# Two streams at two stage transitions: by-token norms, context scaled on VectorE and added on GpSimd, x's products first

## The chip, the core and the metric

The kernel runs on one core of a Trainium2 chip. The metric is the device time of one execution in microseconds (us), the median of three runs. A core has five engines that matter here, each with its own instruction queue: TensorE (PE, matmuls; its weight loads are shown apart as PEld), VectorE (DVE), ScalarE (ACT), GpSimd (POOL) and SyncE (SP, which here only issues the DMAs that load weights). They are ordered among each other by semaphores alone. SBUF holds the operands, PSUM (eight banks of 128 x 512 fp32) the results of matmuls. `fp32r` is the split format in which the kernel makes its matmul operands.

## The reference

Two transformer blocks in fp32, one after the other, on one sequence of 512 tokens with 1024 features. The change lies in the second block, which has two streams: `x` (512 tokens) and `ctx` (256 tokens), with the same weights but gains of their own. Cut to what matters (`shf`, `scf` are a shift and a scale per feature, made from the condition vectors; `_x` and `_c` are the two streams'):

```python
# layer 0
yx, yc = conv_module(hx, ...), conv_module(hc, ...)
x   = x   + g_x * rmsnorm(yx, norm_g[0, 1])        # post-norm and residual
ctx = ctx + g_c * rmsnorm(yc, norm_g[0, 1])
fx = rmsnorm(x,   norm_g[0, 2]) * (1 + scf_x) + shf_x   # next norm
fc = rmsnorm(ctx, norm_g[0, 2]) * (1 + scf_c) + shf_c
x   = x   + gf_x * rmsnorm((silu(fx @ w1) * (fx @ w3)) @ w2, norm_g[0, 3])
ctx = ctx + gf_c * rmsnorm((silu(fc @ w1) * (fc @ w3)) @ w2, norm_g[0, 3])
# layer 1
hx = rmsnorm(x,   norm_g[1, 0]) * (1 + sc_x) + sh_x
hc = rmsnorm(ctx, norm_g[1, 0]) * (1 + sc_c) + sh_c
# keys, values: hx and hc @ wk, wv;   queries: hx @ wq;   then attention, post-norm, ffn of x alone
```

## The kernel before, in words

Activations stand transposed: features on the 128 partitions in KD = 8 chunks, tokens along the free axis (`X` is 8 x 512, `XC` 8 x 256). Every matmul operand is split into a high and a low fp32r part, and each product is made of three matmuls (lines 435 to 437: high weights by high activations, high by low, low by high). A weight matrix is cut into slabs, 1024 rows by 128 columns as a rule. SP loads a slab into one of three `raw` buffers, ACT makes `Wh` from it (L2090), and DVE (L1313) or POOL (L2592) makes `Wl = raw - Wh`; `by_pool` says which. There are three `Wh`/`Wl` pairs, so a slab's `Wh` waits until the products of the slab three before it are done. `ahead(key)` on ACT and DVE makes the parts up to two slabs ahead of `key`.

All five programs are written out by hand as Python functions that emit instructions in order; no scheduler moves them. So an instruction waits for all that stands ahead of it on its engine, and PE's order is that of the calls.

Two places have this form, and are called transition 1 (convolution module to the ffn of layer 0) and transition 2 (that ffn to the attention inputs of layer 1):

1. The post-norm. PE sums the squares of y (`norm_stats`), a root is taken by token: PE leaves one number per token and partition (`token_stat`, L569: the squares are the stationary operand, a column of ones the moving one, so each of the matmuls has one column), ACT and DVE work on 128 x 4 numbers (`small`, L2138, L2141, L1383 to L1392), and PE spreads them again with transposes (`token_rows`, L581) into a "row" in PSUM. `fill_in=(1, 4)` puts one matmul of no use (128 x 512, `keep_warm`, L625) before the transposes and four behind.
2. DVE scales y by row and gain (L1410) and adds it to X (L1481), chunk after chunk, first x's eight, then ctx's eight (`post_norm`).
3. The next norm. ACT squares the new X (L2125) as its chunks come, then ctx's; there are two `sq` buffers. PE sums them with `stat` (L557: ones as the stationary operand, 512 or 256 columns), so the sum comes out spread over all partitions, and the root is taken on 128 x 512 numbers (DVE, four instructions over 512 columns). WARM_AFTER adds four `keep_warm` matmuls.
4. `norm_to_h`: DVE scales chunk c of X (L1410), ACT adds the shift and rounds (L2163, `Hh`), DVE takes the low part (L1427, `Hl`). Then the same for ctx (`hc_h`, `hc_l`).
5. `linear_pair_both`: PE makes the products of the first two slabs with x, chunk by chunk as `Hl` comes, then those with ctx. The third slab and the others follow by `linear_both`, x and ctx in turn.

In the attention inputs (jobs k2_0, k2_1, v2_0, v2_1, then q2_0 to q2_7) each key and query slab is followed on PE by `head_stat` (L557 and L911, the swapped pairs for the rotation). DVE does the rotation (L1681 to L1685), the head's root (L1383 to L1392), the scaling (L1706) and the low parts (L1731, L1736), and ahead of each the `Wl` of a later slab. At transition 0 (into the convolution) the kernel already has the by-token norm for both streams and `linear_trio_both`, which makes three slabs' products with x before any with ctx.

Of the kernel before, what the change touches and what calls it, by code (L numbers as in the profile page):

```python
# [24 lines left out]
P = 128  # L25
# [68 lines left out]
def write(nc, a, out, tally):  # L94
# [285 lines left out]
    WARM = 8  # L380

    def by_pool(key):

        return key[0] in BLOCK_1_SLABS or key[0:2] == ("dn", 1)
# [9 lines left out]
    BY_TOKEN = [t for t in SUMMED if t != ("post", ("ffn", 1, "x"))]  # L394
# [3 lines left out]
    def _(pe):  # L398
# [98 lines left out]
        def linear_trio_both(tag, *three_jobs):  # L497
# [16 lines left out]
            for i in range(KD):  # L514
                pe.wait_ge(*ready("h_low", tag, i))
                for job, w in ws:
                    products(job, w, i, "x")
            take(*three_jobs[2])
# [9 lines left out]
            tally.h_reader[0] = ws[2][0]  # L528

# [70 lines left out]

        def norm_stat(tag, c, n):
# [15 lines left out]


# [146 lines left out]
        def ffn_both():  # L765

            tag, w2 = ("f", 0, "x"), a["ffn_w2_2"][0]
            for lo, hi in F_GROUPS:
                for f in range(lo, hi):
                    w = {x: a["ffn_w%s_2" % x][0, :, f * P:(f + 1) * P] for x in "13"}  # L770
                    if f == 0:
                        linear_pair_both(tag, *((("up" + x, 0, "x", f), w[x], "split") for x in "13"))
                    else:
                        for x in "13":
                            linear_both(("up" + x, 0, "x", f), w[x], ("f", 0, "c"))
# [17 lines left out]
            token_rows(*(("post", ("ffn", 0, s)) for s in "xc"), fill_in=(1, 4))  # L793
# [31 lines left out]
        def conv_both():  # L825
# [32 lines left out]
            token_rows(*(("post", ("conv", s)) for s in "xc"), fill_in=(1, 4))  # L858
# [22 lines left out]
        def attention_inputs():  # L881
# [3 lines left out]
            linear_pair_both(tag, *((("k2", "x", p), wk(p), "split") for p in range(2)))  # L885
            jobs = attention_jobs
            head_stat(jobs[0])
            for i in range(2, len(jobs) + 1):
# [6 lines left out]
                one = jobs[i - 1]  # L895
                if one[0] == "v2":
# [235 lines left out]
        def gqa_attend():  # L1132
# [63 lines left out]
            token_rows(("post", ("att", "x")), fill_in=(1, 4))  # L1196
# [57 lines left out]
        for s in ("x", "c"):  # L1254
            pre(("f", 0, s), NS[s])
        ffn_both()
        for s in ("x", "c"):
            pre(("n", 1, s), NS[s])
# [26 lines left out]
    def _(dve):  # L1285
# [126 lines left out]
        def norm_to_h(tag, n, g, sh, gains=None, ring="one", rooted=False):  # L1412
# [17 lines left out]
            for c in range(KD):  # L1430
# [6 lines left out]
                if c > 0:  # L1437
                    low(c - 1)
            low(KD - 1)

        def norms_to_h(kind, l, ring="both"):

            for s in ("x", "c"):
                norm_to_h((kind, l, s), NS[s], lambda c: col(2, l, s, 7 if kind == "f" else 6, c),
                          lambda c: col(2, l, s, 3 if kind == "f" else 0, c), ring=ring)
# [56 lines left out]
        def conv_both():  # L1502
# [74 lines left out]
            post_norms(("conv",), 0, 8)  # L1577

        def post_norms(tag, l, what):

            for s in ("x", "c"):
                rstd(("ss", ("post", (*tag, s))), NS[s], D)
            for s in ("x", "c"):
                post_norm((*tag, s), NS[s], YB[:, :, 0:SEQ] if s == "x" else YB[:, :, SEQ:],
                          lambda c: col(2, l, s, what, c), "both")

        def ffn_both():

            norms_to_h("f", 0)
# [22 lines left out]
            post_norms(("ffn", 0), 0, 9)  # L1612
# [75 lines left out]
        def attention_inputs():  # L1688

            norms_to_h("n", 1, "one")  # L1690
# [380 lines left out]
    def _(act):  # L2071
# [88 lines left out]
        def norm_highs(tag, n, sh):  # L2160
# [5 lines left out]
        def norms_to_h(kind, l, ctx_ready):  # L2166
# [3 lines left out]
            norm_to_h(x, SEQ, lambda j: col(2, l, "x", what, j), lambda: squares_of_x(c, CTX, ctx_ready))  # L2170
            norm_to_h(c, CTX, lambda j: col(2, l, "c", what, j))
# [52 lines left out]
        def ffn_both():  # L2224

            norms_to_h("f", 0, lambda c: ready("x_new", ("conv", "c"), c))
# [63 lines left out]
        def attention_inputs():  # L2290

            norms_to_h("n", 1, lambda c: ready("x_new", ("ffn", 0, "c"), c))
# [243 lines left out]
        squares_of_x(("f", 0, "x"), SEQ, lambda c: ready("x_new", ("conv", "x"), c))  # L2536
# [221 lines left out]
```

## Time and profile before

| what | value |
|---|---|
| runs | 3268.11, 3269.18, 3278.44 us; median 3269.18 us |
| the profiled execution | 3274.4 us, of which the span of instructions is 3272.6 us |
| PE busy | 3154.5 us (96%) |
| DVE, ACT, POOL busy | 1568.0 us (48%), 1187.5 us (36%), 816.1 us (25%) |
| mean granted clock of TensorE | 0.985 of 2.4 GHz |

The page adds busy time by engine over the whole span; the chain follows back what ended last. A granted clock of 1.00 is TensorE at 2.4 GHz, 0.50 is 1.2 GHz, and values between are a mean over a stretch that holds both.

### The profile page before, as it was taken

To read this page: it belongs to the slowest core of one execution; us is meant where nothing else is said; L and a number is where in the kernel's file an instruction comes from. 1 tells how busy PE (TensorE), PEld (TensorE's weight loads), DVE (VectorE), ACT (ScalarE), POOL (GpSimd) and SP (SyncE) were. 2 spreads that over 40 slices of the span, in tenths; PEclk is the share of its full clock that TensorE was granted. 3 is DMA by queue.
4 is the path that set the end of the run, shared out by engine and by line. 5 is a ranking of instruction groups with operands and counts; after the bars stand their busy time and mean duration, and the time that the engine had idled before them with its cause. 6 is when DMAs were issued, how large, how long until landed. Compare 5 with 4: busy or idle time off the path is not lost.

```text
span 3272.6 us, 38617 instructions
## 1 busy us (share of the span) xinstructions
PE 3154.5 (96%) x15540; PEld 2480.0 (76%) x15540; DVE 1568.0 (48%) x2208; ACT 1187.5 (36%) x1764; POOL 816.1 (25%) x401
## 2 busy tenths in 40 slices
PE   6999999999999999999999899999999979999998
PEld 4657778887765777778877578888888658878887
DVE  3572146464376113333388644322334889653234
ACT  3443244243454223324321343111112558632223
POOL 4302436555320333444400000000000039400000
PEclk9999999999999999999999999999999989999999
DMA  6413436665430555463334211222221110122332
GB/s 238 128 43 110 143 95 194 213 200 165 129 116 1 169 178 167 144 191 92 95 103 121 53 49 55 65 65 65 65 64 52 40 38 1 39 71 87 106 89 79
DMA packets 429892, 337.21 MB, mean 103 GB/s; under 512 B 16637, under 2 KB 411223, under 8 KB 417428
## 3 DMA queue, kind: packets, MB, share of 16 engines
q1 hardware_dynamic: 428272, 334.23, 33.4%
q8 instruction: 124, 2.03, 0.2%
q0 software_dynamic: 1248, 0.46, 0.1%
q14 instruction: 52, 0.43, 0.0%
q10 hardware_dynamic: 196, 0.07, 0.0%
HBM read 319.58 MB, written 2.10 MB: 98 GB/s over the span
## 4 chain that ended last, share of the span: by engine, by line
PE 61%; DVE 5%; ACT 2%; issue 1%; SPq 1%; DMA 0%; POOL 0%; DVEq 0%; ACTq 0%
PE PS L435 17%; PE PS L436 17%; PE PS L437 17%; PE PS L871 1%; PE PS L557 1%; PE PS L1175 1%; PE PS L625 1%; PE PS L1144 1%; PE PS L670 1%; PE PS L1155 1%; PE PS L1176 1%; SPq L2681 1%; DVE both_tmp L1410 1%; DVE X L1481 0%; PE PS L569 0%
## 5 line engine op out<-in xcount | busy, mean ns | idle before, releaser
L435 PE MATMUL PS<-Hh,Wh 128*128 128x512 f32 x2208 | 874.9, 396 | 9.2 <-DVE Hl L1427 5.2
L2592 POOL TENSOR_TENSOR Wl<-raw,Wh 128x1024 fp32r<-128x1024 f32 (+2 forms) x254 | 617.8, 2441 | 989.6 <-ACT Wh L2090 989.6
L436 PE MATMUL PS<-Hl,Wh 128*128 128x512 f32 x2208 | 861.6, 390 | 0.0
L437 PE MATMUL PS<-Hh,Wl 128*128 128x512 f32 x2208 | 861.4, 390 | 0.0
L2090 ACT ACTIVATE Wh<-raw 128x1024 fp32r<-128x1024 f32 (+2 forms) x442 | 436.3, 988 | 394.5 <-PE PS L437 346.9
L435 PEld LDWEIGHTS PS<-Hh,Wh 128*128 128x128 f32 x2208 | 415.8, 188 | 116.7 <-issue 51.9
L437 PEld LDWEIGHTS PS<-Hh,Wl 128*128 128x128 f32 x2208 | 415.6, 188 | 87.9
L436 PEld LDWEIGHTS PS<-Hl,Wh 128*128 128x128 f32 x2208 | 416.0, 188 | 67.9 <-issue 3.4
L1313 DVE TENSOR_TENSOR Wl<-raw,Wh 128x1024 fp32r<-128x1024 f32 (+3 forms) x188 | 217.6, 1157 | 386.9 <-ACT Wh L2090 386.4
L1995 DVE SCALAR_TENSOR_TENSOR cv<-PS,vcols,cv 128x510 f32<-128x510 f32 (+1 forms) x176 | 123.7, 744 | 217.1 <-ACT cv L2511 217.1
L435 PE MATMUL PS<-g_h,Wh 128*128 128x512 f32 x528 | 206.7, 391 | 3.5 <-POOL Wl L2592 3.5
L2624 POOL CAST k_hi<-k_ctx 64x512 fp32r<-64x512 f32 x4 | 4.2, 1044 | 813.2 <-DVE k_ctx L1410 813.0
L437 PE MATMUL PS<-g_h,Wl 128*128 128x512 f32 x528 | 205.5, 389 | 0.0
L436 PE MATMUL PS<-g_l,Wh 128*128 128x512 f32 x528 | 205.5, 389 | 0.0
L435 PE MATMUL PS<-hc_h,Wh 128*128 128x256 f32 x576 | 162.7, 282 | 0.6 <-DVE hc_l L1469 0.5
L436 PE MATMUL PS<-hc_l,Wh 128*128 128x256 f32 x576 | 161.8, 281 | 0.0
L437 PE MATMUL PS<-hc_h,Wl 128*128 128x256 f32 x576 | 161.8, 281 | 0.0
L2639 POOL TENSOR_SCALAR p<-p,small 128x768 f32<-128x768 f32 x64 | 140.5, 2218 | 49.7 <-DVE small L2047 49.7
L557 PE MATMUL PS<-sq,cst 128*128 128x512 f32 (+2 forms) x228 | 111.0, 601 | 32.5 <-DVE stat_v L1383 16.2
L2511 ACT ACTIVATE cv<-PS,vcols 128x512 f32<-128x512 f32 x88 | 68.7, 780 | 191.8 <-PE PS L437 188.6
L435 PEld LDWEIGHTS PS<-hc_h,Wh 128*128 128x128 f32 x576 | 108.1, 188 | 21.9 <-DVE hc_l L1469 1.7
L436 PEld LDWEIGHTS PS<-hc_l,Wh 128*128 128x128 f32 x576 | 108.1, 188 | 19.9
(384 smaller groups left out, 4785.3 us busy)
## 6 DMA issues: line engine op xcount, KB each, us to landing
raw<-in_ffn_w SPq DMA_DIRECT2D x108, 512.0 KB, 3.6
mod_w<-in_w_mod SPq DMA_DIRECT2D x48, 1024.0 KB, 5.0
raw<-in_w_up SPq DMA_DIRECT2D x88, 512.0 KB, 4.7
mod_w<-in_w_ada SPq DMA_DIRECT2D x40, 1024.0 KB, 4.9
raw<-in_w_in SPq DMA_DIRECT2D x62, 512.0 KB, 3.9
UQ<-U SPq DMA_DIRECT2D x128, 99.4 KB, 2.2
raw<-in_w_down SPq DMA_DIRECT2D x32, 384.0 KB, 5.1
raw<-in_conv_w_pw SPq DMA_DIRECT2D x24, 512.0 KB, 4.2
```

Source lines behind the costliest of these rows:

```text
L435: pe.matmul(o, wh, xh, start=start, stop=False, skip_group_check=True)
L436: pe.matmul(o, wh, xl, start=False, stop=False, skip_group_check=True)
L437: return pe.matmul(o, wl, xh, start=False, stop=stop, skip_group_check=True)
L557: mm = pe.matmul(bank(job, n), const(matrix)[lo:hi, :], SQ[i][lo:hi, 0:n], start=first, stop=final, skip_group_check=True)
L625: pe.matmul(PS[:, b, :], const("ident"), cst[:, 0:512], start=True, stop=True)
L670: mm = pe.matmul(PS[32 * j:32 * j + b, bank_of[job], :], cact[b][:, r, :], w[:, 512 * j:512 * (j + 1)], start=r == 0, stop=r == KD - 1, sk ...
L1313: dve.tensor_tensor(low, src, high.bitcast(F32), ALU.subtract).then_inc(*mark("w_low", k))
L1995: ins = dve.scalar_tensor_tensor(o, bank(ups[s])[:, 0:SEQ - lag], vec(("w_conv", l), tap * 2 * FC + s * FC + f), o, ALU.mult, ALU.add)
L2090: act.activation(high, src, ACT.Copy).then_inc(*mark("w_high", k))
L2511: act.activation(cv[f % 2][s][:, :], bank(job), ACT.Identity, bias=vec(("b_conv", l), s * FC + f), scale=vec(("w_conv", l), 2 * 2 * FC + s ...
L2592: pool.tensor_tensor(low, src, high.bitcast(F32), ALU.subtract).then_inc(*mark("w_low_pool", one[0]))
L2639: pool.tensor_scalar(p2[n % 5][:, :], p2[n % 5][:, :], ri2[n % 5], None, ALU.mult)\
```

## The change

The roots of the norms that follow at transitions 1 and 2 are taken by token, for x and ctx (`BY_TOKEN`). Each chunk's squares go through PE by themselves (`chunk_stat`: one-column matmuls, in the place of L557). DVE scales ctx's y in place in YB (eight instructions), and POOL adds it to XC (`add_context`). DVE takes x's next norm before ctx's; ACT squares four chunks of ctx ahead of x's `Hh`, four between them, and takes ctx's root behind the sixth. PE takes the last four chunks of ctx between x's products. Three slabs (instead of two) have x's products made first. The third slab's low part is made by POOL (`THIRD_SLABS`). In the attention inputs `head_stat` of k2_1 moves behind the products of v2_1. The post-norms' `fill_in` goes from (1, 4) to (1, 2), at a third place too, the post-norm of the attention; `pre` of the two norms, with its four `keep_warm`, goes.

```diff
-    BY_TOKEN = [t for t in SUMMED if t != ("post", ("ffn", 1, "x"))]
+    BY_TOKEN = ([t for t in SUMMED if t != ("post", ("ffn", 1, "x"))]
+                + [(*t, s) for t in (("f", 0), ("n", 1)) for s in "xc"])
+    THIRD_SLABS = ("up1", 0, "x", 1), ("v2", "x", 0)
 # PE
+        def into(tag, *three_jobs):
+            c_tag = (*tag[:-1], "c")
+            for c in range(KD):
+                chunk_stat(tag, c, "stat")
+            token_rows(tag, fill_in=(0, 0), own_banks=True)
+            for c in range(4):
+                chunk_stat(c_tag, c, "mod")
+            keep_warm(1)
+
+            def after(i):
+                if i in (1, 3):
+                    for c in (i + 3, i + 4):
+                        chunk_stat(c_tag, c, "mod")
+                if i == KD - 2:
+                    token_rows(c_tag, fill_in=(0, 0), own_banks=True)
+
+            linear_trio_both(tag, *three_jobs, after=after)
...
-            token_rows(*(("post", ("ffn", 0, s)) for s in "xc"), fill_in=(1, 4))
+            token_rows(*(("post", ("ffn", 0, s)) for s in "xc"), fill_in=(1, 2))
...
-            linear_pair_both(tag, *((("k2", "x", p), wk(p), "split") for p in range(2)))
+            into(tag, *((("k2", "x", p), wk(p), "split") for p in range(2)),
+                 (jobs[2], a["attn_wv_2"][0, :, 0:P], "split"))
             head_stat(jobs[0])
-            for i in range(2, len(jobs) + 1):
+            for i in range(3, len(jobs) + 1):
...
                 one = jobs[i - 1]
+                if i == 3:
+                    head_stat(jobs[1])
 # DVE
+            post_norm((*tag, "x"), SEQ, YB[:, :, 0:SEQ], lambda c: col(2, l, "x", what, c), "both")
+            for c in range(KD):
+                one = scaled(YB[:, c, SEQ:], YB[:, c, SEQ:], col(2, l, "c", what, c), CTX, r=bank(row, CTX))
+                one.then_inc(*(empty(row) if c == KD - 1 else mark("ctx_scaled", tag, c)))
 # ACT
+            ahead(first_slab(x))
+            squares_of_x(x, SEQ, lambda j: ready("x_new", (*post, "x"), j))
+            root(("ss", x), SEQ)
+            for j in range(4):
+                square_of_c(j)
+            norm_highs(x, SEQ, lambda j: col(2, l, "x", what, j), between)
+            norm_highs(c, CTX, lambda j: col(2, l, "c", what, j))
 # POOL
+            pool.tensor_tensor(low, src, high.bitcast(F32), ALU.subtract).then_inc(*mark("w_low_pool", third))
+            for c in range(KD):
+                pool.tensor_tensor(XC[:, c, :], XC[:, c, :], YB[:, c, SEQ:], ALU.add).then_inc(*mark("ctx_new", post, c))
```

PE at transition 1, before: the post-norm's transposes (L581), fill (L625), squares' sums of x and ctx, fill, first products.

```order
L625 MATMUL PS<-cst 128x512
L581 MATMUL PS<-cst,small 128x128 x6
L625 MATMUL PS<-cst 128x512 x4
L557 MATMUL PS<-sq,cst 128x512 x8
L557 MATMUL PS<-sq,cst 128x256 x8
L625 MATMUL PS<-cst 128x512 x4
L435 MATMUL PS<-Hh,Wh 128x512
```

The same place in the changed kernel (its L591 is `token_stat`, L603 the transposes, L665 the fill).

```order
L665 MATMUL PS<-cst 128x512
L603 MATMUL PS<-cst,small 128x128 x6
L665 MATMUL PS<-cst 128x512 x2
L591 MATMUL PS<-cst,sq 128x1 x32
L603 MATMUL PS<-cst,small 128x128 x4
L591 MATMUL PS<-cst,sq 128x1 x8
L665 MATMUL PS<-cst 128x512
L437 MATMUL PS<-Hh,Wh 128x512
```

Sixteen wide matmuls became 40 of one column (the other eight stand between the products), and of nine fill matmuls four are left.

PE in the attention inputs, before: `head_stat` of k2_1 (its operand is heads_in_144) stands behind v2_0's products and ahead of v2_1's, which are the last three rows' kind.

```order
L437 MATMUL PS<-hc_h_61,Wl 128x256
L557 MATMUL PS<-sq,cst 128x512
L911 MATMUL PS<-heads_in_144,cst 128x512
L435 MATMUL PS<-Hh,Wh 128x512
L436 MATMUL PS<-Hl,Wh 128x512
L437 MATMUL PS<-Hh,Wl 128x512
L435 MATMUL PS<-hc_h_61,Wh 128x256
```

The same pair in the changed kernel: v2_1's products end in the first row, and behind the pair the turns of v2_0 (heads_in_145) follow at once, then q2_0's products.

```order
L439 MATMUL PS<-hc_h_61,Wl 128x256
L579 MATMUL PS<-sq,cst 128x512
L956 MATMUL PS<-heads_in_144,cst 128x512
L968 MATMUL PS<-cst,heads_in_145 128x128 x4
L968 MATMUL PS<-cst,vt_c_137 128x128 x2
L437 MATMUL PS<-Hh,Wh 128x512
```

The rotation's operand of k2_1 now comes one slab later.

## Rows read from the trace of the kernel before

**Rows 1.** The page: busy us of the engines, share of the span, instructions

```profile
PE 3154.5 (96%) x15540; PEld 2480.0 (76%) x15540; DVE 1568.0 (48%) x2208; ACT 1187.5 (36%) x1764; POOL 816.1 (25%) x401
```

**Rows 2.** Chain of waits, transition 1: start us, us, what

```profile
1945.64 1.41 DVE both_tmp L1410 x2
...
1956.94 0.39 DVE both_tmp L1410
...
1967.29 3.43 PE PS L625 x8
1970.73 0.23 PE PS L435
...
1987.27 0.23 PE PS L435
```

**Rows 3.** Chain of waits, transition 2

```profile
2532.26 1.41 DVE both_tmp L1410 x2
2533.67 0.60 DVE X L1481
2534.27 0.66 DVE both_tmp L1410
...
2541.87 0.64 ACT sq L2125
2542.55 2.00 PE PS L557 x4
...
2555.66 0.23 PE PS L435
...
2574.03 0.86 PE PS L911 x2
...
2583.22 0.86 PE PS L557 x2
```

**Rows 4.** Weight loads of one-column matmuls: start us, us, engine, line, shapes, count

```profile
2524.01 0.97 PEld L569 LDWEIGHTS PS<-cst,stat_v 128*128 128x128 f32 x8 [0.58 <-issue]
2525.82 1.78 PEld L569 LDWEIGHTS PS<-cst,sq 128*128 128x128 f32 x8 [0.83 <-ACT sq L2125]
2528.33 0.97 PEld L569 LDWEIGHTS PS<-cst,sq 128*128 128x128 f32 x4
```

**Rows 5.** Windows: stretch, length, busy us of each engine, granted clock, DMA

```profile
2523.30:2527.50 4.20, 3.05 (x19) 2.79 (x19) 1.80 (x3) 1.12 (x3) 0.00 (x0) 0.77 0.00 0
2527.50:2529.20 1.70, 1.70 (x9) 1.70 (x10) 0.65 (x4) 0.47 (x2) 0.00 (x0) 0.50 0.00 0
2532.20:2536.00 3.80, 3.80 (x11) 1.89 (x10) 3.73 (x6) 1.07 (x2) 0.00 (x0) 0.97 0.00 0
2612.00:2614.00 2.00, 2.00 (x6) 1.53 (x5) 1.90 (x4) 1.42 (x3) 0.00 (x0) 0.50 0.00 0
```

**Rows 6.** A root by token: timelines of ACT and DVE, transition 1

```profile
1941.57 0.26 ACT L2138 ACTIVATE small<-PS,cst 128x4 f32<-128x4 f32 x1
...
1942.57 0.16 DVE L1392 SCALAR_TENSOR_TENSOR small<-small 128x4 f32<-128x4 f32 x1
```

**Rows 7.** Timeline of DVE in the attention inputs, with its idle time before

```profile
2584.97 0.69 DVE L1681 TENSOR_TENSOR tmp<-PS,turnS 128x512 f32<-128x512 f32 x1 [2.84 <-PE PS L911]
...
2604.64 1.22 DVE L1313 TENSOR_TENSOR Wl<-raw,Wh 128x1024 fp32r<-128x1024 f32 x1
2607.65 0.69 DVE L1681 TENSOR_TENSOR tmp<-PS,turnS 128x512 f32<-128x512 f32 x1 [1.80 <-PE PS L911]
...
2619.86 0.69 DVE L1681 TENSOR_TENSOR tmp<-PS,turnS 128x512 f32<-128x512 f32 x1 [3.29 <-PE PS L911]
2622.80 1.77 DVE L1386 TENSOR_TENSOR stat_t<-stat_y 128x512 f32<-128x512 f32 x1
```

**Rows 8.** Windows there, later

```profile
2640.00:2660.00 20.00, 18.07 (x66) 11.72 (x64) 19.37 (x28) 10.61 (x16) 0.00 (x0) 1.00 0.27 79
```

**Rows 9.** Groups of POOL by form: shapes, count, busy us, mean ns, idle before

```profile
L2592 POOL TENSOR_TENSOR Wl<-raw,Wh 128x1024 fp32r<-128x1024 f32 x186 | 487.3, 2628 | 842.1 <-ACT Wh L2090 842.1
L2634 POOL TENSOR_TENSOR v_parts<-v_ctx,v_parts 128x256 fp32r<-128x256 f32 x2 | 2.7, 1328 | 0.2
```

More of the change, by code:

```diff
@@ L599, in summed_stat, with chunk_stat @@
                 tally.square_free[ev] = lambda: full(job)
+        def chunk_stat(tag, c, ring="work"):
+            job, ev = ("ss", tag), (tag, c)
+            if c == 0:
+                begin(job, ring)
+            pe.wait_ge(*ready("squares", ev))
+            i = len(tally.squares) % 2
+            tally.squares.append(ev)
+            mm = token_stat(job, SQ[i], NS[tag[-1]], c == 0, c == KD - 1)
+            if c == KD - 1:
+                mm.then_inc(*fill(job))
+                tally.square_free[ev] = lambda: full(job)
+            else:
+                mm.then_inc(*mark("squares_used", ev))
+                tally.square_free[ev] = lambda: ready("squares_used", ev)
         def norm_stat(tag, c, n):
@@ L616, in keep_warm @@
         def keep_warm(count=WARM):
+            if count == 0:
+                return
             b = turn_of["work"]
@@ L857, in conv_both @@
             norm_stats(("post", ("conv", "x")), KD - 1)
-            token_rows(*(("post", ("conv", s)) for s in "xc"), fill_in=(1, 4))
+            token_rows(*(("post", ("conv", s)) for s in "xc"), fill_in=(1, 2))
         def quad_taps(j):
@@ L1438, in norm_to_h @@
                     low(c - 1)
+                if c == KD - 2 and after_6:
+                    after_6()
             low(KD - 1)
[L1441 to L1445, printed above, removed]
         def mod_out(b, l):
@@ L2164, in norm_highs, with norms_to_h, square_of_c, between @@
                    .then_inc(*mark("h_high", tag, c))
-        def norms_to_h(kind, l, ctx_ready):
+                after(c)
+        def norms_to_h(kind, l, post):
             x, c = (kind, l, "x"), (kind, l, "c")
             what = 3 if kind == "f" else 0
-            norm_to_h(x, SEQ, lambda j: col(2, l, "x", what, j), lambda: squares_of_x(c, CTX, ctx_ready))
-            norm_to_h(c, CTX, lambda j: col(2, l, "c", what, j))
+            def square_of_c(j):
+                act.wait_ge(*ready("ctx_new", post, j))
+                square((c, j), XC[:, j, :], CTX)
+            def between(j):
+                if 1 <= j <= 4:
+                    square_of_c(j + 3)
+                if j == 5:
+                    root(("ss", c), CTX)
+            ahead(first_slab(x))
+            squares_of_x(x, SEQ, lambda j: ready("x_new", (*post, "x"), j))
+            root(("ss", x), SEQ)
+            if tally.h_before.get(x):
+                act.wait_ge(*full(tally.h_before[x]))
+            for j in range(4):
+                square_of_c(j)
+            norm_highs(x, SEQ, lambda j: col(2, l, "x", what, j), between)
+            norm_highs(c, CTX, lambda j: col(2, l, "c", what, j))
         def squares_of_x(tag, n, ready_of):
```

52 lines of the change are left out of this document (29 added, 23 removed).

## The prediction

> **What bounds the kernel now.** I read the page first. PE is busy in 96% of the span [rows 1], so a gain must come from PE's waits, its half clock or its extra work, and there is little of each. Then I followed the chain of waits through the two transitions. At transition 1 it leaves PE at 1945.64, where DVE starts the post-norm, and comes back to products at 1970.73, which is 25.1 us; the last 3.43 us are the fill [rows 2]. At transition 2 the same stretch is 2532.26 to 2555.66, 23.4 us [rows 3]. DVE's pairs of L1410 and L1481 take 0.66 + 0.60 = 1.26 us a chunk, so x's post-norm is about 10 us of it, in both kernels. The windows show the clock, and the timeline of DVE shows what comes after: in the attention inputs DVE waits for PE until 2619.86 [rows 7] and from then on sets the pace (busy 19.37 of 20 us [rows 8]). So at transition 2 an earlier first product is worth nothing by itself; what counts is when DVE gets to 2619.86.
>
> **When x's squares are summed.** In the changed kernel PE passes each chunk as four one-column matmuls (eight loads in the trace, L569). At 2.4 GHz eight loads take 0.97 us, at 1.2 GHz 1.78 us [rows 4]. Less the last load's overlap that is a pitch of about 0.9 or 1.7 us a chunk, and for ctx's four loads (0.97 us at 1.2 GHz) 0.45 or 0.85. Against DVE's 1.26 us a chunk all hangs on the clock. The row that decides for me: from 2527.50 to 2529.20 PE is busy 1.70 of 1.70 us with such loads and their matmuls, and the granted clock is 0.50; in the 4.20 us before, mostly the same work, it fell (mean 0.77). It was back near 1.00 in the window with the four wide fill matmuls [rows 5]. I take it that the clock falls some 3 us behind the last wide matmul and stays at half over the rest of the sums. The Trainium skill (TensorE: Matmul & The Clock Gate, Part 1: The HAM clock gate) says that the gate goes by how busy the array has lately been. Taken at PE's busy share it would keep 2.4 GHz here; the row just named disagrees, and what it would give is rival A.
>
> At transition 2 two fill matmuls (0.86 us each, from 3.43 for four [rows 2]) behind 2532.4 end at 2534.1. Adds of X end 1.26 us apart from 2534.27, a square takes 0.64 more [rows 3]: chunks 0 and 1 are summed at full clock, chunk 2 starts at 2537.6, and six chunks at 1.7 us end at S = 2547.8. Before, the sums ended with the L557 at 2542.55 + 2.00 = 2544.55, so this is 3.2 us later. At transition 1 the fill begins at half clock and lasts longer; chunks 0 to 2 go at full clock, and five more from 1952.1 give S = 1960.6.
>
> **From S to the first product.** ACT's logarithm to DVE's root, by token: 1941.57 to 1942.57 + 0.16, so 1.2 us [rows 6], plus 0.1 of semaphore; before, this was four DVE instructions of 512 columns. Then PE at half clock: four transposes (0.85), four chunks of ctx (3.4), one fill matmul (1.7). The sum is 7.3 us. ACT's third and fourth squares of ctx wait for PE in there and x's first `Hh` waits behind them, but they end by S + 5.9 and are covered by the fill. Some 1.4 us of products at half clock lose half: 0.7 (0 to 2 us; the four restarts that I saw differ). So T' = S + 8.0: 1968.6 at transition 1, 2.1 us earlier than 1970.73; 2555.8 at transition 2, 0.1 us later than 2555.66. The row of x, its `Hh` and `Hl` on DVE are ready before. The cover for DVE's eight ctx scalings (3.1 us, from 0.39 each [rows 2]) is PE's slow sums; without it (rival A) they end 0.1 us before the root is due.
>
> **POOL.** The third slab's low part costs 2.63 us and lies beside x's post-norm, before any use. Eight adds of 256 columns are not in the trace: from 0.66 us each (a quarter of the 1024-column form, 2.63) to 1.33 us [rows 9]. I take the latter, the nearer shape. Eight are 10.6 us; the fourth, which ACT's fourth square needs, is ready 5.3 us after DVE's first scaling and so before S. Cost 0 (0 to 1 us). POOL's reads beside DVE can slow DVE: 1.77 us for an instruction that takes 0.69 otherwise [rows 7], but that hits DVE while it waits for PE's sums.
>
> **Transition 1, the sum.** Before, from 1970.73 to the third slab 16.5 us, and 8.3 for that slab (as v2_0 took, from 2574.03 + 0.86 to 2583.22 [rows 3]): 24.8. After, from T': 48 products with x at 0.227 us = 10.9 (a matmul of the chain shows 0.23 [rows 2]); four sums of ctx and two transposes between them 2.1 (1.8 and 0.3); 24 with x 5.5; 72 with ctx at half the columns 8.5. Together 27.0. ACT's root of ctx stands ahead of its seventh `Hh` and waits for PE's third stop; I find `Hl` 6 ready just as PE asks for it. Slab four needs the first pair's buffer: table load 1.28, gate 0.91, `Wh` 1.04, `Wl` 1.23 are 4.5 us against 5.7 us of products, so no stall. Net: -2.1 + 2.1 = 0.0 us.
>
> **Transition 2, the sum.** The trio ends at T' + 27.0, `head_stat` of k2_0 takes 0.86 + 0.86 [rows 3], v2_1 8.3, `head_stat` of k2_1 1.7. DVE's rotation of k2_1 thus starts at T' + 38.8; before, it started at 2584.97, which is T + 29.3. Behind it on DVE, in the order of the program: rotation, root and scaling 5.4, low parts of k2_0 2.8, `Wl` 1.2, v2_0 1.3, low parts of k2_1 2.8, `Wl` 1.2, v2_1 1.3, root of ctx's key 2.3, `Wl` 1.2: 19.6 us. It is also the stretch from 2584.97 to 2604.64 + 1.22 = 2605.86 [rows 7], 20.9 us, less two waits of 0.2 and 1.1 us that are gone because ACT is early. So the rotation of q2_0 starts at T' + 58.4 = 2614.2. Before, it waited for PE and started at 2607.65. That is 6.5 us later, and what follows keeps the distance: PE's sum for ctx's second key waits for DVE's reading of q2_0's bank, then q2_1's `head_stat`, then 2619.86 and DVE's own pace. PE will stand idle for about 2.3 us ahead of q2_1's products and 5 us ahead of q2_2's, the second as before at half clock afterwards (0.50 at 2612 [rows 5]). Net: +6.5 us.
>
> **The third `fill_in`.** Behind the attention PE is at full clock and DVE sets the pace; two fill matmuls fewer give 0 us.
>
> **Sum.** 0.0 + 6.5 = +6.5 on the profiled execution's 3274.4 gives 3280.9. That execution lies 5.2 us above the median of the runs, 3269.2, on which the forecast is put: 3275.7 us, 0.2% slower. A measurement of this kernel can't tell less than about 0.3% (9.8 us) from no change. With a clock loss of 0 to 2 us at each start, the fall of the clock a chunk earlier or later and POOL's 1 us, the forecast's own range is 3271 to 3280.
>
> **Rivals.**
> A. The one-column sums keep 2.4 GHz. Then DVE's pace ends the sums at about 2544.3, S to T' is 5.0 us (transposes 0.45, ctx 1.8, fill 0.86), T' is 2549.3 and 1962.4. Transition 1 gains 8.3 - 2.1 = 6.2; transition 2 has q2_0's rotation at 2607.7, as before, 0. That gives 3263.0. For it: PE is busy throughout; against: rows 5. It is also what the skill's rule at its word would make.
> B. DVE's queue in the attention inputs does not bind, because it is ahead by more than I count (its waits before were 2.84 and 1.80 us [rows 7]). Then transition 2 costs T' + 2.1, so 2.2 us: 3271.4.
> C. Slower than before: in the trio the one-column sums between x's products keep the clock at half until the pair is done. PE then takes 10.9 us more at each transition, DVE's `Hl` are no help, and transition 2 passes it on through k2_1: 3275.7 + 21.8 = 3297.5. It decides once the clock comes back more than 3.3 us later than I assume at both. Against: 12 wide products stand between two stops, and the clock rose with fill matmuls alone.
> D. The change doesn't do what it says: ctx's adds on POOL or the trio change nothing that is waited for, both transitions keep their length: 3269.
>
> **Chances.** Forecast 0.55, A 0.13, B 0.13, C 0.11, D 0.08. Faster by over 0.3% (under 3259.4) would need A and more at transition 2: 0.07. Slower by over 0.3% (above 3279.0): C and the upper edge of the forecast, 0.20. The same: 0.73. Range: 3263 (A) to 3281.
>
> **What the profile will show.** If the sums run at half clock: eight loads of a chunk 0.21 us apart from the third or fourth chunk on, granted clock 0.5 there, and x's first product 23 to 24 us after DVE's start of the post-norm at both transitions (25.1 and 23.4 before). If DVE's queue binds: PE waits for `Wl` of q2_1 and for DVE ahead of q2_2, and the rotation of q2_0 starts 82 us after the post-norm's start, in place of 75.4. The forecast is wrong if the first products come within 18 us, or if DVE waits for PE ahead of q2_0's rotation; it would be wrong for an unknown reason if the attention's products take another time than before.

## The result, and the profile after

The changed kernel takes 3279.88 us (median of 12 runs, 3278.38 to 3284.75), the kernel before 3273.94 in the same session (12 runs, 3268.11 to 3280.09). The ratio is 1.0021, with an interval of 1.0013 to 1.0029: 6.9 us slower, between 4.3 and 9.5. The difference of the two medians is 5.9 us. The forecast was 3275.7 us, a change of less than 0.3%, so the class is right. The time is 4.2 us above the forecast and lies 0.1 us inside the forecast's own range (3271 to 3280).

Executions of one kernel differ by several us in what lies ahead of the change: with identical code up to there, VectorE (DVE) starts the post-norm of transition 1 anywhere from 1941.4 to 1950.3 us in the traces of this case. So I compare stretches inside a trace. The first is from the start of DVE's post-norm to the second product of the gate (the `both_tmp` of L1598 before, L1641 after); the second from the same start at transition 2 to the rotation of q2_0, and on to the reduction of the first scores.

The lines have moved: L569 is L591 now, L581 L603, L625 L665, L911 L956, L1681 L1724. The chain of waits of the changed kernel at transition 1, in the columns of [rows 2]:

```profile
1941.44 1.41 DVE both_tmp L1451 x2
...
1947.94 8.71 PE PS L591 x40
...
1958.15 1.09 PE PS L603 x4
1959.24 3.21 PE PS L591 x16
1962.44 1.92 PE PS L665 x2
1964.36 0.43 PE PS L437
```

and at transition 2, beside [rows 3]:

```profile
2529.72 1.41 DVE both_tmp L1451 x2
...
2534.96 10.41 PE PS L591 x48
...
2546.70 1.08 PE PS L603 x4
2547.79 3.20 PE PS L591 x16
2550.99 1.92 PE PS L665 x2
```

Over the sums DVE has left the chain; it comes back only for the root. PE's one-column sums are in the chain with six chunks in a piece at transition 2 (eight entries a chunk): 10.41 / 6 = 1.74 us a chunk, where DVE delivers one every 1.26. Behind the root PE is in the chain again, with transposes, four chunks of ctx and one fill matmul. The clock of these stretches, as the granted clock of each window (columns as in [rows 5]):

```profile
1948.00:1952.00 4.00, 4.00 (x19) 4.00 (x20) 4.00 (x8) 1.65 (x3) 0.00 (x0) 0.50 0.00 0
...
1965.00:1970.00 5.00, 5.00 (x21) 4.13 (x20) 2.27 (x4) 1.03 (x3) 0.00 (x0) 0.69 0.01 3
2541.00:2545.40 4.40, 4.36 (x21) 4.27 (x21) 2.02 (x6) 0.64 (x2) 4.40 (x8) 0.50 0.00 0
2553.00:2555.00 2.00, 2.00 (x6) 1.52 (x6) 2.00 (x4) 0.72 (x1) 0.00 (x0) 0.50 0.00 0
2555.00:2560.00 5.00, 5.00 (x27) 4.23 (x26) 2.54 (x5) 1.95 (x4) 0.00 (x0) 0.98 0.00 0
```

PE is busy throughout and stands at 1.2 GHz over the sums, over the work behind the root and into the products: x's first product is at 1964.36 at transition 1 and at 2552.91 at transition 2, and at transition 1 the clock comes back near 1968.1 (mean 0.69 over 1965 to 1970). VectorE in the attention inputs, beside [rows 7], and GpSimd (POOL):

```profile
2582.89 0.69 DVE L1724 TENSOR_TENSOR tmp<-PS,turnS 128x512 f32<-128x512 f32 x1 [3.65 <-PE PS L956]
...
2592.90 0.69 DVE L1724 TENSOR_TENSOR tmp<-PS,turnS 128x512 f32<-128x512 f32 x1 [3.36 <-PE PS L956]
...
2612.14 0.68 DVE L1724 TENSOR_TENSOR tmp<-PS,turnS 128x512 f32<-128x512 f32 x1
...
2622.75 0.69 DVE L1724 TENSOR_TENSOR tmp<-PS,turnS 128x512 f32<-128x512 f32 x1 [1.70 <-PE PS L956]
...
2682.95 1.81 DVE L2077 TENSOR_REDUCE small<-PS 128x1 f32<-128x768 f32 x2
```

```profile
2528.40 2.35 POOL L2678 TENSOR_TENSOR Wl<-raw,Wh 128x1024 fp32r<-128x1024 f32 x1 [570.81 <-ACT Wh L2132]
2540.36 5.51 POOL L2681 TENSOR_TENSOR XC<-XC,YB 128x256 f32<-128x256 f32 x8 [9.61 <-DVE YB L1451]
```

The first five rows are the rotations of k2_0, k2_1, q2_0 and q2_1, and the first scores. Before, DVE waited for PE ahead of q2_0's rotation; now that row has no idle time, and 19.24 us of DVE's own work without a wait lie between the rotation of k2_1 and it. The stretches of all profiled executions, in us, with the runs beside them (a ratio of 0.001 is 3.3 us):

| kernel | T1: to the gate's second product | T2: to q2_0 | T2: to scores | T1 and scores against before | ratio to before, interval |
|---|---|---|---|---|---|
| before | 58.25 | 75.39 | 146.48 | | |
| changed | 60.39 | 82.42 | 153.23 | +8.9 | 1.0021, 1.0013 to 1.0029 |
| changed_again | 60.57 | 82.53 | 153.35 | +9.2 | 1.0034, 1.0022 to 1.0046 |
| t1_only | 60.41 | 76.47 | 147.57 | +3.3 | 1.0019, 1.0010 to 1.0029 |
| t2_only | 58.24 | 82.70 | 154.41 | +7.9 | 1.0013, 1.0004 to 1.0022 |
| early_heads | 60.53 | 77.58 | 148.66 | +4.5 | 1.0016, 1.0008 to 1.0025 |
| wide_sums | 57.19 | 78.95 | 149.78 | +2.2 | 1.0007, 0.9998 to 1.0016 |
| wide_early | 56.45 | 74.71 | 145.80 | -2.5 | 0.9981, 0.9972 to 0.9991 |
| wide_warm | 55.21 | 77.68 | 148.55 | -1.0 | 0.9988, 0.9979 to 0.9998 |
| mended | 55.21 | 72.72 | 143.83 | -5.7 | 0.9976, 0.9967 to 0.9986 |
| mended_again | 55.22 | 72.74 | 143.59 | -5.9 | 0.9971, 0.9959 to 0.9982 |
| split_adds | 53.69 | 71.17 | 142.01 | -9.0 | 0.9968, 0.9956 to 0.9981 |

What follows the first scores, up to VectorE's last instructions, takes 585.7 to 586.6 us in every kernel. From the gate's second product to the start of transition 2 it is 524.1 to 528.4 us, without relation to the edits, and the start differs as told above. That is why a ratio and its row's sum of stretches may differ by 4 us. A stretch isn't exact either. Transition 2 of t1_only is the kernel before's and took 1.1 us longer than there: from 2552 to 2556 its mean granted clock was 0.60, and 1.00 in the trace before. Transition 1 is the same code in wide_sums and wide_early and differs by 0.7 us; the run of the wide sums shows why.

### The profile page after: what moved, and what is told of

Read it like the earlier page. It is cut to its first block, busy times and chain, and to the rows that moved or that the text cites. A ratio compares the mean times of both kernels' runs of the same rounds, so it can differ in the third digit from the quotient of the medians.

```text
span 3276.9 us, 38848 instructions
## 1 busy us (share of the span) xinstructions
PE 3155.7 (96%) x15656; PEld 2495.9 (76%) x15656; DVE 1555.8 (47%) x2190; ACT 1181.7 (36%) x1764; POOL 831.8 (25%) x419
## 4 chain that ended last, share of the span: by engine, by line
PE 58%; DVE 5%; POOL 4%; ACT 1%; issue 1%; SPq 1%; DMA 0%; POOLq 0%; DVEq 0%; ACTq 0%
PE PS L437 17%; PE PS L438 17%; PE PS L439 17%; POOL p L2712 4%; PE PS L913 1%; PE PS L591 1%; PE PS L710 1%; SPq L2754 1%; PE PS L665 0%; PE PS L579 0%; DVE q_parts L1778 0%; DVE both_tmp L1451 0%; PE PS L1111 0%; DVE stat_t L1427 0%; DVE Wl L1354 0%
## 5 line engine op out<-in xcount | busy, mean ns | idle before, releaser
L437 PE MATMUL PS<-gb_h,Wh 128*128 128x512 f32 x352 | 120.1, 341 | 1.9 <-DVE gb_l L1506 1.9
```

The source lines that it names most:

```text
L437: pe.matmul(o, wh, xh, start=start, stop=False, skip_group_check=True)
```

## Experiments

Two theories were to be told apart from rivals: the half clock (PE's one-column sums bring the clock down, and what stands behind them pays), and VectorE's queue (a late statistic of k2_0 and k2_1 leaves DVE idle first and 19 us of its own work late afterwards).

**Each transition alone.** The other one is the kernel before's, on all engines.

The diff shows the start of t1_only's edit; t2_only keeps the other half.

```diff
-    THIRD_SLABS = ("up1", 0, "x", 1), ("v2", "x", 0)
+    THIRD_SLABS = (("up1", 0, "x", 1),)
...
-                + [(*t, s) for t in (("f", 0), ("n", 1)) for s in "xc"])
+                + [(*t, s) for t in (('f', 0),) for s in "xc"])
...
```

> The changed kernel with the change at the first transition alone (conv to feed-forward); the second transition, into the attention inputs, is the kernel before's. Theory: the traces of before and after put +1.7 us at this transition (start of VectorE's post-norm to start of the next one 586.6 before, 588.3 after), because PE runs the one-column sums and the first nine products at half clock; so about 3275.6 us, +1.7 on the kernel before. The prediction on record said 0.0 for this place. Rival (the whole loss is one common cost, the half clock, shared evenly by both places): +3.5. Rival (this place gains, and the second one loses more): -2 or less.

> The changed kernel with the change at the second transition alone; the first is the kernel before's. Theory: +6.7 us on the kernel before, about 3280.6, as the stretch from VectorE's post-norm to the first scores grew from 146.5 to 153.2 us, nearly all by the late rotation of k2_1 and VectorE's queue of 19 us behind it. With the first-transition run the two should add up to the whole change, +6.9. Rival (even split): +3.5.

Measured: 3279.32 us against 3273.49 for t1_only, and 3276.46 for t2_only. Both times miss what was expected: by the ratios it is +6.2 us where +1.7 stood, and +4.3 where +6.7 stood. The first miss lies outside the interval. The intervals (+3.3 to +9.5 us, +1.3 to +7.2 us) are too wide to say which transition costs more. The traces can:

```profile
1948.15 1.41 DVE L1450 SCALAR_TENSOR_TENSOR both_tmp<-YB,der,PS 128x512 f32<-128x512 f32 x2 [1.69 <-PE PS L603]
...
2008.56 0.95 DVE L1655 TENSOR_TENSOR both_tmp<-both_gate,PS 128x768 f32<-128x768 f32 x1 [6.27 <-PE PS L439]
```

is t1_only, 60.41 us for 58.25, and

```profile
2528.84 1.41 DVE L1451 SCALAR_TENSOR_TENSOR both_tmp<-YB,der,PS 128x512 f32<-128x512 f32 x2 [1.68 <-PE PS L603]
...
2611.54 0.68 DVE L1739 TENSOR_TENSOR tmp<-PS,turnS 128x512 f32<-128x512 f32 x1
```

is t2_only: no idle time ahead of q2_0, 82.7 us after the start. The new form costs 2.2 us at transition 1 and 6.7 to 7.9 at transition 2, whatever stands at the other one. The 7.9 are t2_only's: behind a wait of 3.6 us PE ran at a granted clock of 0.50 from 2616 to 2620 there, and at 1.00 in that place in the changed kernel. The times of t1_only lie 3 us above what its stretches give, which I can't explain beyond the spread ahead of the change.

**The statistics of two heads earlier.**

```diff
-            head_stat(jobs[0])                   # behind the trio
+   then=lambda n: n == 1 and head_stat(jobs[0]) # in the trio, behind k2_1's ctx
+            head_stat(jobs[1], "mod")            # ahead of v2_1's products
...
-                if i == 3:
-                    head_stat(jobs[1])           # behind v2_1's products
```

> The changed kernel with the two heads' statistics of the second transition put earlier on PE: that of k2_0 behind k2_1's ctx products, ahead of v2_0's, and that of k2_1 right behind v2_0's, ahead of v2_1's 48 products, in the other statistics bank. Nothing is left out. Theory (late statistics of k2_0 and k2_1 keep VectorE idle, then its own queue binds until q2_0): rotation of k2_0 2.6 us earlier, of k2_1 about 6 earlier (57 us after the post-norm's start for 63.2), of q2_0 76 to 77 after it for 82.4, and the time 5.5 to 6 us less than the changed kernel's, about 3274. Rival (VectorE isn't what binds, PE's products are late by the half clock at the head): PE's v2_1, q2_0 products stand where they stood or 1.3 us later, q2_0's rotation at 82 still, 3279 to 3280.

```profile
2533.93 1.41 DVE L1450 SCALAR_TENSOR_TENSOR both_tmp<-YB,der,PS 128x512 f32<-128x512 f32 x2 [1.68 <-PE PS L604]
...
2584.38 0.69 DVE L1723 TENSOR_TENSOR tmp<-PS,turnS 128x512 f32<-128x512 f32 x1 [0.82 <-PE PS L955]
...
2590.96 0.68 DVE L1723 TENSOR_TENSOR tmp<-PS,turnS 128x512 f32<-128x512 f32 x1
...
2611.51 0.69 DVE L1723 TENSOR_TENSOR tmp<-PS,turnS 128x512 f32<-128x512 f32 x1 [1.25 <-PE PS L955]
```

k2_1's rotation comes 57.03 us after the start (63.18 in the changed kernel) without a wait, q2_0's at 77.58, and DVE waits for PE ahead of it again. The scores are 4.6 us earlier. The medians, 3277.45 and 3279.88, are 2.4 us apart and from two sessions, so the time of about 3274 that was expected did not come, and only the trace gives the size. By it VectorE's idle time ahead of the two rotations cost 4.6 of the 6.7 us. What is left against the kernel before, 2.2 us, is PE's: PE was busy in all 54 us from 2556 to 2610 of this trace.

**Wide sums.** The same loads and the same number of matmuls, 128 columns of ones for one; the root is read from every 128th column of PSUM (not in the cut).

```diff
-   mm = pe.matmul(PS[:, bank_of[job], t:t + 1], part[:, t * P:(t + 1) * P], const("ones", 0, 1),
+   w = W if job[1] in WIDE else 1               # W = 128
+   mm = pe.matmul(PS[:, bank_of[job], t * w:(t + 1) * w], part[:, t * P:(t + 1) * P], const("ones", 0, w),
```

> The changed kernel with the sums over squares of both new norms as before by token, the same count of products with the same stationary blocks, but with 128 columns of ones as moving operand in place of one (512 columns of PSUM a chunk), and the root read from every 128th column. Nothing is left out. Theory (the clock falls to 1.2 GHz because one-column products leave the array nearly idle, and everything behind them is paid at that clock until it returns): granted clock 1.00 through the sums, loads 0.97 us to eight... x's chunks at their squares' pace (under 1.2 us) and not 1.7, x's sums done 12 to 13 us after the post-norm's start for 15.7, the first product 17 to 18 us after it for 23; about -6 us at the first transition and -5 to -7 at the second: 3266 to 3269. Rival (wide moving operands aren't hidden behind the block loads: 4 x 0.43 us a chunk at full clock): chunks of 1.7 us, no gain, 3279. Rival (the clock gate isn't decided by columns but by the engine waiting for squares): clock 0.50 as before and chunks of 3.4 us, 3295 or more.

Windows, and weight loads of the sums at transition 2:

```profile
1948.00:1952.00 4.00, 3.57 (x25) 2.90 (x24) 4.00 (x8) 2.09 (x4) 0.00 (x0) 1.00 0.21 70
...
2537.00:2541.00 4.00, 3.70 (x28) 3.12 (x28) 4.00 (x9) 2.27 (x4) 0.69 (x1) 1.00 0.01 2
2545.00:2548.00 3.00, 2.69 (x13) 2.72 (x14) 1.56 (x3) 0.42 (x1) 0.82 (x2) 0.50 0.02 5
```

```profile
2539.95 1.86 PEld L599 LDWEIGHTS PS<-cst,sq 128*128 128x128 f32 x16 [0.29 <-ACT sq L2175]
2545.28 0.71 PEld L611 LDWEIGHTS PS<-cst,small 128*128 128x128 f32 x4 [3.46 <-issue]
```

From 1948 to 1952 PE is less busy than with one column (3.57 for 4.00 us), and the granted clock is 1.00 instead of 0.50. The window begins 3.3 us after the post-norm's start here and 6.6 us after it in the changed kernel; the second row begins 7.3 us after the start, deep in the sums, and shows the same. The Trainium skill (TensorE: Matmul & The Clock Gate, Part 1: The HAM clock gate) has the clock set by how busy the PE has been; by the profile's busy time these two rows contradict it, since the busier stretch has the lower clock. The wider operand costs nothing that the trace shows: two chunks in a row take 1.86 us, 0.93 each, as eight loads took 0.97 [rows 4]. The sums go at DVE's 1.26 us a chunk again and end 12.15 us after the start (2541.8) for 15.65. But my expectation for the first product (17 to 18 us) and for the time (3266 to 3269) was missed: it came at 20.6 us at transition 2 and 21.4 at transition 1, and the time is 3273.84, the same as the kernel before's within the interval. The second load row says why. PE loaded nothing for 3.46 us while the root was made, and ctx's chunks behind it ran at 0.50 in the last window. The root itself was late as well. Its four instructions on DVE, from the timeline of the changed kernel, where the first of them waited for ACT:

```profile
2545.69 0.16 DVE L1424 TENSOR_SCALAR small<-PS 128x4 f32<-128x4 f32 x1 [2.67 <-ACT small L2180]
2546.00 0.17 DVE L1427 TENSOR_TENSOR small<-small 128x4 f32<-128x4 f32 x1
...
2546.39 0.16 DVE L1433 SCALAR_TENSOR_TENSOR small<-small 128x4 f32<-128x4 f32 x1
```

and with the wide sums:

```profile
2540.54 2.44 DVE L1459 SCALAR_TENSOR_TENSOR YB<-YB,der,PS 128x256 f32<-128x256 f32 x6
2542.89 0.16 DVE L1432 TENSOR_SCALAR small<-PS 128x4 f32<-128x4 f32 x1
2543.08 0.72 DVE L1435 TENSOR_TENSOR small<-small 128x4 f32<-128x4 f32 x1
...
2544.51 0.65 DVE L1441 SCALAR_TENSOR_TENSOR small<-small 128x4 f32<-128x4 f32 x1
```

From the last sum to the root's end it is 1.2 us there (2545.37 to 2546.55) and 3.4 us here (2541.81 to 2545.16). Of the 2.2 us more, 0.8 are the scalings of ctx that DVE still had to finish, and 1.4 are in three instructions of four columns that take 0.65 to 0.72 us and not 0.17. GpSimd's eight adds lie beside them (2540.31 to 2545.81 in this trace); in the changed kernel they were over. The run with split adds, below, tests that.

The 0.8 us by which transition 1 is later than transition 2 are GpSimd's too. DVE's first addition of X took 1.52 us there, where the others take 0.68:

```profile
1946.01 1.52 DVE L1526 TENSOR_TENSOR X<-X,both_tmp 128x512 f32<-128x512 f32 x1
```

GpSimd made the third slab's low part beside it (from 1944.63, 2.35 us). At transition 2 of this trace that was over before DVE's first addition. In wide_early it is the other way round: 0.69 us at transition 1, and 1.49 at transition 2 (2531.82) beside the low part that starts at 2530.41. This explains the 0.7 us between the two kernels' stretches at transition 1.

**Both edits, the fill moved, and all three.** wide_early has the first two. wide_warm has the wide sums and the fill moved, mended all three:

```diff
-            token_rows(tag, fill_in=(0, 0), own_banks=True)
+            token_rows(tag, fill_in=(3, 0), own_banks=True)
             for c in range(4):
                 chunk_stat(c_tag, c, "mod")
-            keep_warm(1)
```

> The changed kernel with both edits measured before, each alone: 128 columns of ones in the sums over squares, and the statistics of k2_0 and k2_1 earlier. Theory: the two losses are separate terms, so the stretches should add. First transition as with the wide sums alone, 57.2 us from VectorE's post-norm to the second product of the gate (before 58.25, changed kernel 60.39). Second: q2_0's rotation at 74 us after the post-norm (before 75.4, changed 82.4, wide alone 79.0, early alone 77.6), first scores at 145 (before 146.5, changed 153.2). Time 2 to 3 us under the kernel before, about 3271. Rival (one cause seen twice: either edit takes the same idle time): q2_0 at 77, 3273 to 3274.

> The wide sums with the filling matmuls moved: three between x's last sum and the transposes of its root, where PE stood idle for 3.5 us, and none behind ctx's first four chunks, where one lay on the path with 0.86 us. Theory (PE falls to 1.2 GHz in the root's gap, so that ctx's four chunks take 3.0 to 3.2 us and not 1.6): granted clock 1.00 there, ctx's chunks in 1.6 to 1.8, first product 1.3 to 2 us earlier than with the wide sums alone (18.6 to 19.3 us after the post-norm's start for 20.5), both transitions shorter by that; 3270. Rival (x's h is late on ACT and VectorE anyway, the gap only moves): first product within 0.4 of 20.5 and no change, 3273.8.

> All three edits: wide sums, early statistics, fill in the root's gap. Nothing is left out. Theory (terms add): first transition 55.5 to 56 us, q2_0's rotation 72.5 to 73 us after the post-norm, scores at 143.5 to 144; 5 us under the kernel before, 3268.5. Rival (VectorE is next to bind: its 1.34 us for each pair of h operations holds the products' pace): at most 1 us on the run with two edits, 3270 to 3271.

wide_early: 3268.07 us, q2_0 at 74.71, scores at 145.80; the terms add within 0.8 us, and the time is 3 us better than expected. wide_warm: 3268.88 us, first product 19.2 us after the start (2542.73 - 2523.51), as expected. mended: 3264.82 us against 3274.70 (0.9976, 0.9967 to 0.9986), and 20 us under the changed kernel of the same session, where that one was 5 us slower than in its first session; by the stretches it is 14.6 us. Its chain at transition 2 and a window of it:

```profile
2540.38 0.62 PE PS L611 x4
2541.00 0.46 PE PS L599 x4
2541.55 0.40 ACT sq L2173
...
2542.41 0.62 ACT Hh L2211
2543.06 0.76 DVE Hl L1474
```

```profile
2541.00:2544.00 3.00, 2.10 (x18) 1.75 (x16) 2.35 (x4) 2.37 (x5) 0.00 (x0) 1.00 0.00 0
```

Transposes take 0.62 us for 1.08, the clock stays at 1.00, and the first product now waits for ACT's squares of ctx, x's `Hh` and DVE's `Hl`, no longer for PE.

**GpSimd's adds split.** In mended, the last four adds wait until x's root is made.

```diff
             for c in range(KD):
+                if c == 4:
+                    pool.wait_ge(*ready("stat_r", root_of))
...
-            token_rows(tag, fill_in=(3, 0), own_banks=True)
+            token_rows(tag, fill_in=(2, 0), own_banks=True)
```

> The kernel with all three edits, with GpSimd's last four adds of ctx held back until VectorE has made x's root, and two filling matmuls in the root's gap for three. In the traces with the wide sums three of the root's four instructions on VectorE (four columns each) take 0.72, 0.65 and 0.65 us while GpSimd adds beside them, and 0.16 to 0.17 in the changed kernel, where GpSimd was done by then. Theory (GpSimd's adds slow VectorE's small instructions): they take 0.17 again, the first product comes 1.3 to 1.5 us earlier (17.8 us after the post-norm's start for 19.2), both transitions are shorter by 1 to 1.5 us (54 and 142.5 for 55.2 and 143.8), and the time is 2 to 3 us less than with three edits, about 3262. Rival (they are slow for another reason, as the scalings just ahead of them on VectorE): 0.65 to 0.72 still, first product at 19.2, 3265.

> The kernel with all three edits once more, beside the one with split adds. Theory: stretches 55.2, 72.7 and 143.8 us within 0.3, the time 3265 to 3267, 0.997 to 0.998 of the kernel before. Rival (its lead of 0.24% was an accident of the executions): over 0.999.

```profile
2538.57 0.15 DVE L1430 TENSOR_SCALAR small<-PS 128x4 f32<-128x4 f32 x1
2538.76 0.16 DVE L1433 TENSOR_TENSOR small<-small 128x4 f32<-128x4 f32 x1
...
2539.15 0.16 DVE L1439 SCALAR_TENSOR_TENSOR small<-small 128x4 f32<-128x4 f32 x1
```

```profile
2535.99 2.78 POOL L2689 TENSOR_TENSOR XC<-XC,YB 128x256 f32<-128x256 f32 x4 [9.61 <-DVE YB L1457]
2539.39 2.79 POOL L2689 TENSOR_TENSOR XC<-XC,YB 128x256 f32<-128x256 f32 x4 [0.62 <-DVE small L1439]
```

With GpSimd silent from 2538.77 to 2539.39 the same instructions take 0.16 us, and DVE's scalings of ctx stand right ahead of them here too. So it was contention, not the scalings. The root's first instruction, which reads PSUM, took 0.16 us beside GpSimd too (2542.89 in wide_sums). The Trainium skill (GPSIMD Engine Reference, 1. Specifications) says that GpSimd's SBUF interfaces are shared with VectorE and that DVE instructions with two SBUF inputs contend for them; these rows agree with it. The first product is 17.7 us after the start (2543.04 - 2525.35), both transitions are 1.5 to 1.8 us shorter than in mended, and the time is 3266.54 us against 3275.09 (0.9968, 0.9956 to 0.9981), the lowest ratio of this case and faster than both kernels. The 1.5 us belong to both edits of this run together: the two fill matmuls end at 2539.41, when the root is just ready (2539.31), and a third would have stood in the way. The expected 3262 us did not come. mended_again has 3265.20 in the same session, which is lower, so the runs don't show the gain of 3 us; the one trace of split_adds shows it at both transitions, against both traces of the mended kernel. mended_again repeats the stretches of mended within 0.25 us.

**The changed kernel again.**

> The changed kernel once more, beside the mended ones on one chip, since executions of one kernel differ by 3 us in what lies ahead of the change. Theory: the stretches repeat within 0.3 us (60.4 and 153.2), the time is 3278 to 3281. Rival (the losses are a matter of the execution, not of the change): one of the two stretches is as in the kernel before, 58.25 or 146.5.

Both stretches repeat within 0.2 us, and the median is 3284.79 us (5 runs), above what I expected. Its trace starts transition 1 at 1950.07, where the first one had 1941.44. The stretches belong to the change; the 5 us between the two medians don't.

**VectorE's queue, doubled.** The four subtractions for k2_0's low parts are done twice, with the same result.

```diff
-                for e in range(2):
+                for n in range(8 if g == 0 else 4):
```

> The changed kernel with the four subtractions of k2_0's low parts on VectorE done twice (four more, 0.59 to 0.69 us each, 2.7 us), between the rotations of k2_1 and q2_0. Theory (in the changed kernel VectorE's own queue sets q2_0's rotation): q2_0's rotation 2.7 us later, 85.1 us after the post-norm's start for 82.4 and 82.5. Rival (PE's q2_0 statistics set it): 82.4 still, the doubled work in VectorE's idle time.

> The same doubling in the kernel with all three edits, where VectorE had idled 1.24 us for PE ahead of q2_0. Theory: 1.24 us of the 2.7 are hidden, q2_0's rotation at 74.2 us for 72.7, and the next one, which had idled 3.3 us for PE, where it was (84.95 after the start). Rival (VectorE binds there too): q2_0 at 75.4 and the next one later by as much.

In the changed kernel:

```profile
2529.93 1.41 DVE L1451 SCALAR_TENSOR_TENSOR both_tmp<-YB,der,PS 128x512 f32<-128x512 f32 x2 [1.68 <-PE PS L603]
...
2615.24 0.68 DVE L1724 TENSOR_TENSOR tmp<-PS,turnS 128x512 f32<-128x512 f32 x1
```

That is 85.31 us, 2.9 later, all of the added work (four instructions of 0.69 us), and the first scores are 2.9 us later too. In the mended kernel:

```profile
2526.95 1.41 DVE L1457 SCALAR_TENSOR_TENSOR both_tmp<-YB,der,PS 128x512 f32<-128x512 f32 x2 [1.68 <-PE PS L611]
...
2601.19 0.68 DVE L1730 TENSOR_TENSOR tmp<-PS,turnS 128x512 f32<-128x512 f32 x1
...
2613.41 0.69 DVE L1730 TENSOR_TENSOR tmp<-PS,turnS 128x512 f32<-128x512 f32 x1 [3.32 <-PE PS L962]
```

q2_0 is at 74.24 us for 72.72, so 1.2 of the 2.7 us were hidden, as the theory says. The next rotation I expected where it was, at 84.96; it came at 86.46, 1.5 us later, with 3.32 us of idle time ahead of it as before. This one rotation is a poor measure: in mended_again, the same kernel as mended, it came at 83.36 with 1.70 us of idle time, because PE ran at full clock behind its wait (1.00 over 2606.8 to 2610.8; in mended 0.65 over 2600 to 2604). The first scores settle it: they come at 145.32 us, against 143.83 and 143.59, so about 1.6 of the 2.7 us came through. Each of the two doublings is one execution. So idle time of DVE there is little slack: PE's sum for ctx's second key waits until DVE has read q2_0's bank (2.71 us in the mended kernel, 3.57 here), and q2_1's products and statistics stand behind it. Each waits for the other in turn, and a delay goes round.

## Why the prediction was right, and where it wasn't

**Half clock in the sums: right.** Forecast 1.7 us a chunk and x's sums done 15.5 us after the start of transition 2; measured 1.74 and 15.65. wide_sums shows that it is the one column: on PE nothing else was changed.

**The first product.** With the 0.7 us of later products taken off, the forecast was 22.3 and 22.8 us after the start of transitions 1 and 2; measured 22.9 and 23.2. Of the 0.7 and 0.4 us, the fill (1.92 us for 1.7) and the transposes (1.09 for 0.85) have 0.5, the sums and the root the rest, and ctx's chunks were 0.2 quicker (3.2 for 3.4).

**Products at half clock: mis-sized at transition 1.** The term was 0.7 us. There x's first nine products ran at a pitch of 0.43 us, from 1964.36 to 1968.2, for 0.23 at full clock, which loses 1.8 us. From the first product to the gate's second, wide_sums, at 1.00 over 1965 to 1968, takes 35.8 us and the changed kernel 37.5, a difference of 1.7. So this step fell short by 1.0 us. At transition 2 six products ran slow and the loss was 1.2 us. The forecast took its 1.4 us of slow products as an average of restarts and named 0 to 2 us as the bounds of the loss.

**The trio's sum at transition 1: 0.5 us short.** From the first product to the second of the gate wide_sums takes 35.8 us at full clock, the kernel before 33.1 (58.25 - 25.1): 2.6 us more where the sum had 2.1. With the first product's 0.7 us and the clock's 1.0 that makes the whole miss: forecast 0.0, measured +2.1.

**VectorE's queue at transition 2: right.** Forecast: k2_1's rotation 62.3 us after the start, then 19.6 us of queue, q2_0 at 82; measured 63.2, 19.24 and 82.4. The rotation was 0.9 us later than forecast for the reasons above, and the shorter queue hid 0.4 of it. Forecast +6.5 us, measured +6.7 at the scores. early_heads takes 4.6 of it back and double_low passes all added work on. PE's idle time came out at 2.2 us ahead of q2_1's products (forecast 2.3), but at 3.25 ahead of q2_2's (forecast 5).

**POOL: cost right, price wrong.** The adds take 0.69 us each (5.51 / 8), not 1.33, and lie beside PE's slow sums. The prediction's other price, a quarter of the 1024-column form, was the right one. The 1.33 us of [rows 9] are no property of the shape: the same two instructions took 0.89 us on average in the changed kernel, one 1.06 and one 0.72. The contention that the prediction named hits DVE "while it waits for PE's sums", as it said; without the slow sums it costs 1.4 us at each transition, which no case of the forecast had. The third slab's low part was to cost nothing beside x's post-norm; it costs 0.8 us where it overlaps DVE's first addition of X (wide_sums at transition 1, wide_early at transition 2).

**The third `fill_in`: right.** Behind the first scores the kernel before takes 585.8 us and the changed kernel 585.9.

**Rivals.** A (the clock holds) is what wide_sums makes of the kernel; as that kernel shows, A's price was too good too: at transition 1 it gains 1.1 us, not 6.2 (1.8 in wide_early, where GpSimd's low part is out of the way), because the clock falls in the root's gap and the root is 2.2 us late by DVE's scalings and GpSimd's adds. A had the scalings end 0.1 us before the root is due; in wide_sums they held it up by 0.8. A's 5.0 us from the sums to the first product are also more than its own terms, which with the root's 1.3 give 4.4. With those mended (split_adds) the first product is at 17.7 us, where A had 16.8, and transition 1 is 4.6 us shorter than before. B is excluded by double_low. C asked for 10.9 us at each transition; the clock was back 3.8 us after the first product at transition 1, and near 2555, 2 us after it, at transition 2. D is excluded by the stretches, which are both longer.

**The sum.** +2.1 and +6.7 make 8.9 us in the trace, the runs say 6.9 (4.3 to 9.5), the forecast had 6.5. That the median of the changed kernel lies 4.2 us above the forecast comes from the base: the kernel before had 3269.2 in three runs and 3273.9 in twelve, 4.8 us more. So the good agreement of 6.5 with 6.9 is in part luck: the spread of what lies outside the two stretches hid the 2.1 us of transition 1 that the sum lacked. The prediction also took less than 0.3% to be beyond measuring; twelve executions of each kernel gave 0.21% with an interval of 0.13 to 0.29%.

## What to carry to other kernels

Before a wide matmul is thinned to one column to save work, look at what the engine does to its own clock: here the saving was lost in the sums and in the 10 to 12 us behind them, and 128 columns under the same weight loads cost nothing. When a statistic is moved behind more products, count the queue of the engine that waits for it: with 6.2 us of VectorE's idle time ahead of 19 us of its work taken out (early_heads), the first scores came 4.6 us earlier. Where runs of one kernel differ by 5 us upstream, a 2 us term is measured between two events of one trace, not by medians.

## What the runs showed of the hardware

- The granted clock followed the moving operand's width at the same loads: 0.50 with one column and PE 4.00 of 4.00 us busy, 1.00 with 128 columns and 3.57 of 4.00.
- The clock was also at 0.50 behind 3.46 us in which PE loaded nothing for the root (2545 to 2548 in wide_sums), and stayed at 1.00 with three fill matmuls of 0.86 us in that gap.
- DVE instructions of four columns take 0.16 us alone and 0.65 to 0.72 beside GpSimd's adds, and those of 512 columns 0.69 alone and 1.65 to 1.77 beside its work on ctx's keys; but the first of the root's four, which reads PSUM, took 0.16 beside GpSimd too.
- Behind the same wait of PE of 2.71 us, the same kernel ran on at a mean granted clock of 0.65 in one execution (mended) and at 1.00 in another (mended_again), which moved the next rotation by 1.6 us and the first scores by 0.2.
- GpSimd adds 128x256 in f32 in 0.69 us. A 128x256 subtraction of it that writes fp32r took 1.06 and 0.72 us in the changed kernel and 1.33 on average before [rows 9], so its price moves with what runs beside it.
